# Attention items by token tile, gate products on 256 columns, and the first and last expert-weight loads in halves, in a two-layer attention and mixture-of-experts kernel

## The reference, cut to what matters

```python
for layer in range(2):                       # x: (1, 256, 1024) float32, 16 heads of 64
    mix = nsa_mixer(x, ...) if layer == 0 else moba_mixer(x, ...)
    x = layer_norm(DN_ALPHA * x + mix, ...)
    x = layer_norm(DN_ALPHA * x + grouped_moe(x, ...), ...)
# nsa_mixer: three causal branches, weighed per token and head
proj = h @ w_in                              # q, six key/value groups, gates (48 columns)
g = jax.nn.sigmoid(gates).reshape(B, S, 3, N_HEADS, 1)
o = g[:, :, 0] * heads(o_cmp) + g[:, :, 1] * heads(o_slc) + g[:, :, 2] * heads(o_win)
# moba_mixer: at 256 tokens one block, so plain causal attention with 16 heads
# grouped_moe: 16 experts of width 512, two of them for each token
he = jax.nn.silu(xt @ w_gate[e]) * (xt @ w_up[e]);  out = out + (he @ w_down[e]) * gate[:, e:e + 1]
```

## Time and profile before

| | before |
|---|---|
| median of three executions | 806.09 us |
| the profiled execution: its time, its span | 809.25 us, 807.4 us |
| TensorE busy | 757.7 us (94%) |
| VectorE, ScalarE, GpSimd busy | 282.3, 187.8, 88.0 us |
| mean DMA rate | 303 GB/s |
| granted clock, mean | 0.963 |

### The profile page before, as it was taken

The page is one execution under the profiler, slowest core; times in us unless marked ns, Lnnn a source line. Parts: engine busy times, 40 slices in busy tenths (PEclk is TensorE's granted clock), DMA queues, the critical chain, the costliest instruction groups (busy, mean ns, idle before and its releaser), DMA issues.

```text
span 807.4 us, 9035 instructions
## 1 busy us (share of the span) xinstructions
PE 757.7 (94%) x3713; PEld 404.5 (50%) x3713; DVE 282.3 (35%) x564; ACT 187.8 (23%) x435; POOL 88.0 (11%) x96
## 2 busy tenths in 40 slices
PE   6999999998999999999896999899899999999894
PEld 4877865545534434443235888455633444434331
DVE  3585255425312112111127776432611211211114
ACT  3443355502101011001003444622111100110000
POOL 0011134403000000000000221321200000000000
PEclk9999689999999999999997999999899999999997
DMA  9999500016599999999999944212669999999991
GB/s 301 365 394 379 231 2 1 1 52 242 190 431 428 428 427 426 428 426 427 425 397 387 400 160 157 105 53 98 267 251 429 427 427 427 429 427 427 427 388 54
DMA packets 39500, 245.03 MB, mean 303 GB/s; under 512 B 5408, under 2 KB 9632, under 8 KB 26656
## 3 DMA queue, kind: packets, MB, share of 16 engines
q1 hardware_dynamic: 39456, 244.41, 74.8%
HBM read 243.35 MB, written 1.05 MB: 303 GB/s over the span
## 4 chain that ended last, share of the span: by engine, by line
PE 80%; DMA 8%; DVE 7%; ACT 3%; issue 2%; DVEq 0%; SPq 0%
PE ps L644 24%; PE ps L665 12%; DMA ring<-in_w_up 7%; PE ps L594 7%; PE ps L467 5%; PE ps L468 5%; PE ps L469 4%; PE ps L634 3%; PE ps L675 3%; ACT R L983 2%; PE ps L504 2%; PE ps L516 2%; PE ps L625 1%; PE ps L607 1%; PE ps L450 1%
## 5 line engine op out<-in xcount | busy, mean ns | idle before, releaser
L644 PE MATMUL ps<-ring,R 128*64 128x512 f32 x928 | 230.0, 603 | 5.3 <-DMA ring<-in_w_gate 5.3
L644 PEld LDWEIGHTS ps<-ring,R 128*64 128x64 f32 x928 | 72.2, 139 | 115.9 <-issue 114.0
L665 PE MATMUL ps<-ring,R 128*64 128x512 f32 x448 | 113.4, 596 | 0.8 <-DMA ring<-in_w_down 0.8
L1118 DVE TENSOR_TENSOR wl<-ring,wh 128x512 fp32r<-128x512 f32 x88 | 66.5, 770 | 50.0 <-ACT wh L859 49.7
L881 ACT ACTIVATE wh<-ps,small 128x512 fp32r<-128x512 f32 x32 | 22.0, 687 | 263.6 <-PE ps L665 262.1
L467 PE MATMUL ps<-wh,xh 128*128 128x512 f32 x176 | 72.7, 413 | 4.9 <-DVE wl L1118 4.8
L468 PE MATMUL ps<-wl,xh 128*128 128x512 f32 x176 | 71.2, 405 | 0.0
L469 PE MATMUL ps<-wh,xl 128*128 128x512 f32 x176 | 71.0, 403 | 0.0
L665 PEld LDWEIGHTS ps<-ring,R 128*64 128x64 f32 x448 | 35.4, 137 | 67.4 <-issue 63.5
L859 ACT CAST wh<-ring 128x512 fp32r<-128x512 f32 x88 | 54.2, 621 | 59.9 <-PE ps L469 59.9
L1289 DVE SCALAR_TENSOR_TENSOR wl<-ps,small,wh 128x512 fp32r<-128x512 f32 x32 | 24.0, 751 | 105.5 <-ACT wh L881 104.8
(11 more groups left out here) (156 smaller groups left out, 893.6 us busy)
## 6 DMA issues: line engine op xcount, KB each, us to landing
ring<-in_w_gate SPq DMA_DIRECT2D x32, 2048.0 KB, 19.1
ring<-in_w_up SPq DMA_DIRECT2D x26, 2048.0 KB, 18.9
ring<-in_w_down SPq DMA_DIRECT2D x24, 2048.0 KB, 19.5
ring<-in_w_in SPq DMA_DIRECT2D x22, 1024.0 KB, 14.1
R<-in_w_up SPq DMA_DIRECT2D x6, 2048.0 KB, 22.3
ring<-in_w_out SPq DMA_DIRECT2D x8, 1024.0 KB, 15.0
R<-in_w_down SPq DMA_DIRECT2D x4, 2048.0 KB, 20.0
ring<-in_w_down SPq DMA_DIRECT2D x8, 1024.0 KB, 28.1
```

The costliest lines, as they stand in the source:

```text
L644: last = mm(ps[64 * e:64 * e + 64, to, :], xe[:, j, at + 64 * e:at + 64 * e + 64], slots[e][:, j * UNIT:(j + 1) * UNIT], start=(j == 0), s ...
L665: last = mm(ps[64 * e:64 * e + 64, 2 + w, :], hT[:, k, 64 * e:64 * e + 64], slots[e][:, at:at + UNIT], start=(k == 0), stop=(k == FJ - 1))
L1118: tt(wl[:, c % WBUF], in_slot(("unit", u))[:, j * UNIT:(j + 1) * UNIT], wh[:, c % WBUF], ALU.subtract).then_inc(w_lo, 1)
```

## The change

There are three edits.

**Gates.** The high and low parts of the gate weights lie side by side, 64 columns each, padded with zeros (`gate_w`, two of the weight buffers), and stand in the array, while xh and xl stream through as 256 columns. That makes 16 products (2 inputs, 8 depth slices), whose result is transposed: gates by tokens, high part over low part. The ScalarE copies it (`gate_T`), and two products with a doubled identity (`both`) add the two parts and turn them back. The VectorE gets a memset and an addition.

**Attention items.** An item is now four blocks of one token tile: in layer 0 two heads times both branches, in layer 1 four heads. The counts stay 16 and 8; even items are tile 0 (128 keys), odd items tile 1 (256 keys). Each item has one maximum, four exponentials, one scaling, and one copy of the transposed probabilities, on the VectorE alone. The mask is added only where it is not zero. Probabilities of tile 0 have one buffer and those of tile 1 two.

```diff
             def scores(l, m):
-                jq, br, jk, _ = ITEMS[l][m]
+                t, n = m % T, (m % T + 1) * P
...
-                banks = [2 * (m % 2) + a for a in range(2)]
+                to = [ps[:, 2 * t + a, 0:2 * n].rearrange("p (b k) -> p b k", b=2) for a in range(2)]
                 for a in range(2):
-                    mm(ps[:, banks[a], 0:3 * P], identb[:, :], causalb[:, :], start=True, stop=False, skip_group_check=True)
-                for t in range(T):
-                    at, n = t * P, (t + 1) * P
+                    mm(to[a][:, :, t * P:n], identb[:, :], bc(causalb[:, :], 1, 2), start=True, stop=False, skip_group_check=True)
+                if l == 0:
+                    jq = m // T
                     for a in range(2):
-                        last = mm(ps[:, banks[a], at:at + n], qT[half_[a], jq, t * P:(t + 1) * P],
-                                  kT[half_[a], jk, 0:n], start=False, stop=True, skip_group_check=True)
+                        last = mm(to[a], qT[half_[a], jq, t * P:(t + 1) * P], kT[half_[a], jq // 4:jq // 4 + 3:2, 0:n],
+                                  start=False, stop=True, skip_group_check=True)
...
+                for b, jq in enumerate(heads_of(l, m)):
+                    for k in range(t + 1):
+                        for a in range(2):
+                            c = (256 * b + 64 * (2 * (jq // 4) + a)) if l == 0 else 128 * jq + 64 * a
+                            last = mm(out_of(l, u, b)[64 * a:64 * a + 64, t * P:(t + 1) * P], V[l][:, k, c:c + DH],
+                                      PTb[t][:, a, b, k], start=(t == 0 and b == 0), stop=False, skip_group_check=True)
...
-                    for a in range(T):
                         for j in range(KJ):
-                            for k, (xs, ws) in enumerate(((xh, wh), (xh, wl), (xl, wh))):
-                                cols = ws[:, GATES % WBUF, j * 3 * H:(j + 1) * 3 * H]
...
+                            last = mm(ps[0:P, 2, 0:S], gate_w[:, j].rearrange("p k c -> p (k c)"), xs[:, j, :],
+                                      start=(n == 0), stop=(n == 2 * KJ - 1))
...
-                        copy(PTb[m % 2][:, 0, :], ps[:, 4, 0:3 * P]).then_inc(L.pt_sb, 1)
+                        copy(PTb[m % T].rearrange("p a b k c -> p a (b k c)"), ps[:, 4:6, 0:2 * P * (m % T + 1)]).then_inc(L.pt_sb, 1)
```

```diff
+            def load_halves(n):
+                for h in range(2):
+                    for e in range(2):
+                        what = ("moe", n + e)
...
+                        if h == 0 and k in (3, 4) and i == 1:
+                            sp.wait_ge(main.gate_half, l + 1)
+                        elif h == 0 or i == 1:
+                            slot_free(what)
+                        c = slice(2 * D * h, 2 * D * (h + 1))
+                        sp.dma_start(in_slot(what)[:, c], expert_src(l, 2 * i + k % 2, k // 2)[:, c]
+                                     ).then_inc(landing(what, h)[0], 16)
...
-                for n in range(SLOT + 1, 6 * PAIRS):
+                load_halves(6 * PAIRS * l + SLOT + 1)
+                for n in range(SLOT + 3, LASTROUND):
                     load_expert(6 * PAIRS * l + n)
+                for n in range(LASTROUND, 6 * PAIRS, 2):
+                    load_halves(6 * PAIRS * l + n)
```

More of the change, by code:

```diff
@@ L303, in copies, with probs, heads_of, out_of @@
             return min(n + 1, 6) + (n >= 10) if l == 0 else max(0, n + 1 - 8)
[L307 to L310, removed]
+        ITEMS = [H, H // 2]
+        def probs(m):
+            t = m % T
+            return (P1[m // 2 % 2] if t else P0).rearrange("p (a b k) -> p a b k", a=2, b=2)
+        def heads_of(l, m):
+            u = m // T
+            return [u, u] if l == 0 else [2 * u, 2 * u + 1]
+        def out_of(l, u, b):
+            return ps[:, 6 + u % 2, 0:S] if l == 0 else ps[:, 6 + u % 2, b * S:(b + 1) * S]
         block = ctx.enter_context(nc.Block())
@@ L642, in to_hidden @@
                         pe.wait_ge(*parts[j // 2])
+                    if j == KJ // 2:
+                        if half_done:
+                            last.then_inc(half_done, 1)
+                        for what in second:
+                            pe.wait_ge(*landing(what, 1))
                     for e in range(2):
@@ L696, in experts @@
                                   [((rd.xe, rd.xa)[p % 2], 2 * g + 1 + p // 2) for p in range(4)] if w == 0 and i % 2 == 0
-                                  else ())
+                                  else (), [c for c in chunks[2 * w:2 * w + 2] if in_halves(c)],
+                                  rd.gate_half if i == 0 and w == 0 else None)
                         if w == 0:
@@ L806, in _ @@
                     last.then_inc(w2_done, 1)
+                    pe.wait_ge(gates_t_sb, 1)
+                    for a in range(T):
+                        last = mm(ps[:, 2, S + a * 64:S + a * 64 + 3 * H], gate_T[:, a * P:(a + 1) * P], both[:, 0:3 * H],
+                                  start=(a == 0), stop=True, skip_group_check=True)
+                    last.then_inc(L.proj, 1)
                     transpose_roped(0, 6)
@@ L1165, in attention_max @@
                 dve.wait_ge(L.s_done, B.s_done + m + 1)
[L1166 to L1170 removed]
+                k = (m % T + 1) * P
+                nc.vector.tensor_reduce(nmax[:, m % 2], ps[:, 2 * (m % T):2 * (m % T) + 2, 0:2 * k].rearrange("p a (b k) -> p a b k", b=2),
+                                        AX.X, ALU.max, negate=True).then_inc(L.mx, 1)
             def compressed_less_max():
@@ L1388, in _ @@
                         compressed_copy()
-                    if m >= 4 and (m - 4) % nb == nb - 1:
+                    if m >= 4 and m % T:
                         dve.wait_ge(L.pv, B.pv + m - 3)
-                        jq = (m - 4) // nb
-                        copy(OT[jq], ps[:, 6 + jq % 2, 0:S]).then_inc(L.ot_sb, 1)
+                        u = (m - 4) // T
+                        if l == 0:
+                            copy(OT[u], ps[:, 6 + u % 2, 0:S]).then_inc(L.ot_sb, 1)
+                        else:
+                            copy(OT2[u], ps[:, 6 + u % 2, :]).then_inc(L.ot_sb, 2)
                 half_stats(0, 0, 0, L.mix, B.mix + 1)
```

162 lines of the change are left out of this document (77 added, 85 removed).

## The result

The changed kernel takes 783.51 us (median of 4 runs, 782.36 to 784.76) beside 807.06 for the kernel before on the same chip: a ratio of 0.9702, 95% interval 0.9684 to 0.9720, which is 24.0 us of the 806.09 (22.6 to 25.5). The forecast was 23.2 us. Its profiled execution took 782.36 us, the fastest of the four, with a span of 780.6; that of the kernel before, 809.25 us, lies at the upper end of its range (804.58 to 809.53).

A forecast was written before the change was run, and what follows sets the result against it. The TensorE was taken as the bound (80% of the chain), with DMA also near its limit in the experts. Terms -6.9 - 2.7 - 2.0 - 0.8 - 10.8 = -23.2 us from median 806.09 give about 783 us, range 777 to 790.

The forecast's parts named there:

- Gates, -6.9: Gate products to first mask: sixteen products take 1.9 us instead of 7.8, first mask at 88.9 instead of 95.81, -6.9 us.
- Clock behind them, -2.7: First mask to item 4 of layer 0: item 4 starts 9.6 us earlier, so -2.7 us beside the gates' 6.9.
- two low stretches: Behind the gates: one low-clock stretch over the first two scores and a second behind the compressed ones, as before.
- rival (4): Clock stays full from the gates to the compressed scores: 2 us more gained, 780.9 us; chance 0.09.
- bound -4.7: Limit of the clock term if the low clock does not come ahead of the compressed scores.
- Steady attention, -2.0: Layer 0, items 4 to 14: two items take 6.51 us against 6.90, five pairs, -2.0 us.
- Rival (3): VectorE becomes attention's bound, two items 7.5 us instead of 6.5, with a 1024-column copy above 2 us: 794; chance 0.05.
- Layer 1, -0.8: Layer 1 attention: four pairs give -1.9 us, part returns at the output copy and last values, net -0.8 us.
- Loads, -10.8: Expert weight loads: all last-round waits and their low clock go, 5.9 us in layer 0, 4.9 in layer 1.
- signs of being wrong: VectorE's 1024-column copy far off 1.2 us, low clock at another place, or waits for weights remaining.
- lead of 2.4 us: Expert load stream: early halves start 3.5 us sooner, 1.1 us lost in a hole, so the stream is 2.4 us ahead.
- the 3.5 us that halves give at the end: Last expert round: with tiles in halves, a tile may land 3.5 us later than now without a wait.

The follow-up runs named there:

- the loads alone: The kernel before with only the load edit (early half loads of expert tiles, last round in halves): ratio 0.9903 to the kernel before.
- the attention alone: The kernel before with only the attention edit: ratio 0.9939 to the kernel before.
- the gate edit alone: The kernel before with only the gate edit: ratio 0.9895 to the kernel before.
- the run with four early tiles: The changed kernel with two more expert tiles of each layer loaded in halves, first halves starting at half of the first up products: ratio 0.9700 to the kernel before.
- the run with 0.60 us more: The changed kernel with a needless maximum over 512 columns on the VectorE ahead of each copy of 1024 columns: ratio 0.9793 to the kernel before.
- the coefficients taken out: The kernel with two more tiles in halves, the VectorE computing an even item's coefficients ahead of the next odd item's maximum: 781.20 us, ratio 0.9677 to the kernel before.
- the run without early halves: The changed kernel without the four early half loads at half of the first gate products, last round still in halves: ratio 0.9736 to the kernel before.
- the run with the shared copy: The changed kernel with the copy of an odd item's transposed probabilities shared between VectorE and ScalarE: ratio 0.9746 to the kernel before.

## Why the prediction was right, point by point

The total was forecast at -23.2 us and came at -24.0. That it came so near is in part luck: of its terms one was exceeded by a course to which the prediction gave a chance of 0.09, and another fell short.

- **Gates, -6.9.** Right in size against the profiled execution: 12.75 to 5.60 is -7.15, the sixteen products took 1.89 us, and the ScalarE's two copies ended last. One link was not as walked. The prediction had the ScalarE later than the TensorE by its table load; in the trace the load was done at 85.63 and the ScalarE then waited for the TensorE twice, so the two run level and the load stands in nobody's way. And the size hangs on where the clock fell in the execution before. With the old gates it was 10.93 in the loads alone and 11.08 in the attention alone, and against these it is -5.4.
- **Clock behind them, -2.7.** The step that failed is the first of two low stretches. Low stretches were expected over the first two scores and again behind the compressed ones; the first never came, and one of 3.4 us came behind the compressed ones. That is rival (4). First mask to fifth item gained 4.3 us (bound -4.7): 3.2 from the gate edit alone, 1.1 from the attention edit alone. The term was put down to the clock alone, but a quarter of it is the new cut of the items. The 4.3 us are a good case, too. In the run with four early tiles, whose gates and attention are the changed kernel's, the stretch behind the compressed scores was low for 6.8 us, and first mask to fifth item took 14.32 us instead of 12.84. Against that execution the term is -2.8, the forecast's size by another course than the forecast's.
- **Steady attention, -2.0.** 6.50 us against 6.51, copy of 1024 at 1.22 against 1.19, wait for the VectorE in place of the ScalarE. 1.8 us in five pairs. Rival (3) is out with the 1.22. That the VectorE closes the loop is shown from both sides, by the run with 0.60 us more and by the coefficients taken out.
- **Layer 1, -0.8.** First to last mask -1.9 as said, and the output product waits for the last copy (the TensorE's wait for it was 0.9 us). From the last mask to the last 36 output products it was 16.33 us before and is 17.24, so 0.9 comes back and the term is -1.0. The table's row ahead of the experts shrinks all the same, by 0.6, because the low clock there was 3.4 us shorter. The chain before, and after:

```profile
543.25 15.65 PE ps L594 x36
```

```profile
521.46 0.70 DVE R L1430
522.17 0.04 issue
522.21 15.72 PE ps L623 x36
```

- **Loads, -10.8.** Measured -5.1 and -4.3, so 1.4 us too much, and the waits that remained were one of the prediction's own signs of being wrong. The term that was mis-sized is the lead of 2.4 us. The early halves flowed 4.4 us behind the first gate products, as said. But behind them came a gap at 279 GB/s, and tile 11 landed 23.65 us behind the start of the gate products instead of 24.90, a lead of 1.25 us. By the landings the gap is 1.4 us, and tile 13 landed another 0.5 us late. At that tile the lead is 1.25 us in layer 0 and 0.96 in layer 1 against the kernel before, 1.2 and 1.1 against the run without early halves. With the 3.5 us that halves give at the end, 5.9 was needed to take all waits away, and about 1.0 us of wait stayed. Part of the gap can be read from the issues: a 2 MB load issued to an empty queue landed 8.0 us behind its issue (tile 9 before: 217.22 to 225.27), while in the full stream landings stand 4.9 apart, so to follow without a gap a load must be issued some 3.1 us ahead of its forerunner's landing. Tile 11 was issued 2.9 us ahead in layer 0 and 1.7 in layer 1. That explains 0.2 us of the gap of 1.4 in layer 0 and 1.4 of 2.1 in layer 1; the rest is not resolved. The low clock behind the long wait did vanish: gate products of the last round took 7.04 us.
- **Two misses hid each other**: 1.6 us more at the clock, 1.4 us less at the loads.

## What to carry to other kernels

A row of small products cost twice here, by its starts and by the clock of what stands behind it; turning it so that each product streams many columns paid, even with a transpose back. Where two engines alternate in a loop, write one turn as a chain: the step to move out is one that could have been done while its engine idled (here 0.3 us of coefficients, worth more than half of a 1.2 us copy moved to another engine). And size such terms from several executions, when a low clock stands in the stretch: here one such stretch moved a term by 1.5 to 1.8 us, as much as the misses of the prediction's terms.

## What the hardware showed that was not expected

- Once brought down by 64 products of 64 columns, the clock stayed at 0.50 for 30.7 us, over attention with the TensorE busy for 21.62 of 22 us; with sixteen products of 256 columns it did not fall.
- The same gate code took 12.75 us up to the first mask in one trace and 10.93 in another, by where the fall of the clock came.
- The low stretch behind the compressed scores lasted 3.4 us in the changed kernel's trace and 6.8 in that of the run with four early tiles, with the same code there; it cost 1.5 us.
- A load of 2 MB issued to an empty queue landed 8.0 us behind its issue; in the full stream one landed every 4.9 us.
- In a full queue, a transfer of 1 MB costs 0.04 us more than half of one of 2 MB.
- In mid-stream one tile landed 1.4 us late (the run with the shared copy, layer 1), and the trace shows no cause.
